# Two residual stages and the projection stripe ahead of each, cut into two token halves, in a hybrid decoder step (Trainium2)

## The reference, cut to what matters

```python
def rmsnorm(x, g):
    x32 = x.astype(F32)
    y = x32 * lax.rsqrt(jnp.mean(x32 * x32, axis=-1, keepdims=True) + EPS)
    return (y * g.astype(F32)).astype(x.dtype)
...
    mix = jnp.concatenate([retention_out(ret_o, rg), diff_head_out(d_o, subln_g, lam_init)], axis=-1).astype(x.dtype)
    x = x + rmsnorm(mix @ w_out, g_mix_post)
    x = x + rmsnorm(cross_attn(rmsnorm(x, g_mem_pre), mem_k, mem_v, w_mem_q, w_mem_o), g_mem_post)
    x = x + rmsnorm(sq_relu_mlp(rmsnorm(x, g_mlp_pre), w_up, w_down), g_mlp_post)
```

## Time and profile before

| | |
|---|---|
| median of 3 runs | 2825.09 us (2824.94 to 2826.55) |
| the profiled execution, its own time | 2828.37 us |
| its span in the trace | 2826.8 us |
| PE busy | 2761.9 us, 98% |
| DVE busy | 2123.9 us, 75% |
| ACT busy | 1115.1 us, 39% |
| TensorE clock granted, mean | 0.994 of full |

### The profile page before, as it was taken

How to read it: one execution, slowest core, us unless ns; L and a number is a source line. 1 busy time by engine, 2 the same in 40 slices (tenths; PEclk the granted TensorE clock), 3 DMA queues, 4 the chain that set the end, 5 groups by cost and what they waited for, 6 DMA issues and landing times.

```text
span 2826.8 us, 48374 instructions
## 1 busy us (share of the span) xinstructions
PE 2761.9 (98%) x18594; PEld 2538.4 (90%) x18594; DVE 2123.9 (75%) x2699; ACT 1115.1 (39%) x1412; POOL 275.8 (10%) x444
## 2 busy tenths in 40 slices
PE   7999999999999999898999999999999999999998
PEld 6999999999899999767899999999988888888887
DVE  7788886665566653757877777777789888888886
ACT  8143333333233332444544444444444333333332
POOL 0000001233312100000000000000010000000000
PEclk9999999999999999999999999999999999999999
DMA  7444345566756554332344444444464433545353
GB/s 236 143 124 135 114 131 173 184 194 190 228 186 227 188 193 134 111 110 91 115 154 136 151 141 144 148 144 138 148 194 134 157 119 117 162 129 159 94 180 134
DMA packets 387959, 430.37 MB, mean 152 GB/s; under 512 B 13878, under 2 KB 300844, under 8 KB 385644
## 3 DMA queue, kind: packets, MB, share of 16 engines
q1 hardware_dynamic: 346088, 269.19, 31.9%
q0 software_dynamic: 41504, 159.26, 16.5%
q10 hardware_dynamic: 228, 0.06, 0.0%
HBM read 342.21 MB, written 86.25 MB: 152 GB/s over the span
## 4 chain that ended last, share of the span: by engine, by line
PE 86%; DVE 8%; issue 2%; DMA 2%; ACT 2%; DVEq 0%; SPq 0%; POOL 0%; ACTq 0%; POOLq 0%
PE gemm L2934 24%; PE gemm L3031 5%; PE aux L3031 5%; PE aux L3033 5%; PE aux L3032 5%; PE gemm L3033 5%; PE gemm L3032 5%; PE gemm L3619 3%; PE gemm L3621 3%; PE gemm L3620 3%; PE aux L3621 3%; PE aux L3620 3%; PE aux L3619 3%; PE aux L3077 2%; PE gemm L3630 1%
## 5 line engine op out<-in xcount | busy, mean ns | idle before, releaser
L2934 PE MATMUL gemm<-act_hi,w_hi 128*128 128x288 f32 x1744 | 390.9, 306 | 3.4 <-DVE act_lo L2400 2.6
L2934 PE MATMUL gemm<-act_hi,w_lo 128*128 128x288 f32 x1744 | 374.2, 296 | 0.0
L2934 PE MATMUL gemm<-act_lo,w_hi 128*128 128x288 f32 x1744 | 373.6, 296 | 0.0
L2934 PEld LDWEIGHTS gemm<-act_hi,w_hi 128*128 128x128 f32 x1744 | 279.5, 189 | 32.0 <-issue 22.0
L2934 PEld LDWEIGHTS gemm<-act_hi,w_lo 128*128 128x128 f32 x1744 | 281.4, 189 | 0.0
L2934 PEld LDWEIGHTS gemm<-act_lo,w_hi 128*128 128x128 f32 x1744 | 281.3, 189 | 0.0
L1700 ACT ACTIVATE w_hi<-w_raw 128x2048 fp32r<-128x2048 f32 x60 | 115.1, 1919 | 304.2 <-PE aux L3621 175.5
L2578 DVE TENSOR_TENSOR w_lo<-w_raw,w_hi 128x1024 fp32r<-128x1024 f32 x120 | 146.7, 1222 | 108.3 <-ACT w_hi L1623 108.3
L1811 DVE TENSOR_TENSOR w_lo<-w_raw,w_hi 128x2048 fp32r<-128x2048 f32 x63 | 144.1, 2287 | 45.7 <-ACT w_hi L1197 45.4
L3031 PE MATMUL gemm<-act_hi,w_hi 128*128 128x288 f32 x504 | 149.9, 298 | 6.9 <-DVE w_lo L1982 4.3
L3031 PE MATMUL aux<-act_hi,w_hi 128*128 128x288 f32 x528 | 155.4, 294 | 0.0
(11 more groups left out here) (522 smaller groups left out, 7694.1 us busy)
## 6 DMA issues: line engine op xcount, KB each, us to landing
w_raw<-in_w_mlp_up SPq DMA_DIRECT2D x120, 512.0 KB, 4.3
w_raw<-in_w_mlp_down SPq DMA_DIRECT2D x32, 1024.0 KB, 6.3
side_hi<-in_w_mlp_down SPq DMA_DIRECT2D x32, 1024.0 KB, 7.1
w_raw<-in_w_in SPq DMA_DIRECT2D x29, 1024.0 KB, 6.6
w_raw<-in_w_in SPq DMA_DIRECT2D x54, 512.0 KB, 4.1
w_raw<-in_w_out SPq DMA_DIRECT2D x16, 1024.0 KB, 5.9
u_sum_scratch<-u_sum POOLq DMA_DIRECT2D x32, 512.0 KB, 2.9
z_scratch<-z_out SPq DMA_DIRECT2D x56, 288.0 KB, 2.4
```

Source lines behind the costliest of these rows:

```text
L2934: ins = M(out[half][:, 0:TH], w[b][:, cols], x[:, k, half * TH:(half + 1) * TH], start=first and n == 0, stop=last and n == 2)
```

## The change

The two stages work by token halves: half 0 is tokens 0 to 287, half 1 the rest. In words:

- The last output tiles before a stage (two before stage 0, four before stage 1: `LAST`) are made by halves: first all of them for half 0, then all for half 1 (`last_tiles`). Between the products of half 1 stand the column sums and the `spread` of half 0's row factor.
- `residual` takes these tiles out of PSUM half by half, and then goes through 32 half-chunks (`q` = 0 to 31, sixteen of half 0, then sixteen of half 1) in place of 16 chunks. `scale`, `add`, `low`, the high part and the square work on 288 tokens each. The loops are written out.
- `col_sums` is called for two of the four quarters at a time: 32 calls for x in a stage in place of 16.
- `root`, `recip` and `spread` run once for each half, four times in a stage in place of two, on 64 of the 128 rows. Those for half 1's y, and those for half 0's new x, stand inside the loop.
- The split of the next weight stripe (`lo_halves`, `hi_halves`) moves from ahead of the loop into its first steps. In stage 1 the split of stripe `S_MLP` on DVE is cut in two and stands between the tiles.
- `behind` becomes 10 half-chunks, in both stages.
- SP's waits for x follow the new counts: the loads after stage 0 still begin after the last `add`, and the first store of x in stage 1 waits for 20 of 32 steps.

```diff
-            def first_tiles(k, stripe, tile, behind):
-
-                col_sums(n_y_sum, n_acc, True, False)
+            def y_sums(k, half):
+
+                groups = range(2 * half, 2 * half + 2)
+                pe.wait_ge(n_yacc, SUM0[k] + KC - LAST[k] + (half + 1) * (LAST[k] - 1))
+                col_sums(n_y_sum, n_acc, True, False, groups)
+                pe.wait_ge(n_ysq, SQ0[k] + KC - LAST[k] + (half + 1) * LAST[k])
+                col_sums(n_y_sum, n_sq[1], False, True, groups).then_inc(n_ss, 1)
+
+            def half_part(b, k, cols, out, half, first, last):
+
+                x = slice(half * TH, (half + 1) * TH)
+                M(out[:, 0:TH], w_hi[b][:, cols], act_hi[:, k, x], start=first, stop=False, skip_group_check=True)
+                M(out[:, 0:TH], w_hi[b][:, cols], act_lo[:, k, x], start=False, stop=False, skip_group_check=True)
+                return M(out[:, 0:TH], w_lo[b][:, cols], act_hi[:, k, x], start=False, stop=last, skip_group_check=True)
+
+            def last_tiles(k, stripe, tile0, ks):
+
+                per, width = LAST[k], 2048 // ks
+                pe.wait_ge(s_wlo, stripe + 1)
                 for half in range(2):
...
+                        for kk in range(ks):
+                            if half and i * ks + kk == 4:
+                                y_sums(k, 0)
+                            elif half and i * ks + kk == 10:
+                                spread(4 * k + 1, 0, n_y_bc)
+                            at = kk * width + j % per * P
+                            ins = half_part(stripe % 2, kk, slice(at, at + P), G[2 * (j % 2) + half], half, kk == 0, kk == ks - 1)
+                        ins.then_inc(s_tile if half else n_h0, 1)
+
+            def first_tiles(k, stripe, behind):
...
+                for q in range(2 * KC):
+                    half, c = q // KC, q % KC
+                    if q == 3:
+                        y_sums(k, 1)
+                    elif q == 7:
+                        spread(4 * k + 2, 1, n_y_bc)
+                    elif q == KC + 5:
+                        spread(4 * k + 3, 0, n_x_bc)
+                    pe.wait_ge(n_xsq, 2 * KC * k + q + 1)
+                    col_sums(n_x_sum, n_sq[c % 2], c == 0, c == KC - 1, range(2 * half, 2 * half + 2)).then_inc(n_used, 1)
+                    if q == behind:
+                        pe.wait_ge(s_wlo, stripe + 2)
+                    if q >= behind:
+                        chunk(1, q - behind)
+                    pe.wait_ge(n_lo, 2 * KC * k + q + 1)
+                    ins = chunk(0, q)
                 ins.then_inc(s_tile, 1)
-                for c in range(KC - behind, KC):
-                    ins = chunk(1, c)
+                for q in range(2 * KC - behind, 2 * KC):
+                    ins = chunk(1, q)
                 ins.then_inc(s_tile, 1)
-                spread(2 * k + 2, n_x_bc)
+                spread(4 * k + 4, 1, n_x_bc)
```

DVE's side of the stage:

```diff
+                for q in range(2 * KC):
+                    if q + 2 == KC:
+                        dve.wait_ge(n_bcs, 4 * k + 2)
+                    if q + 2 < 2 * KC:
+                        scale(q + 2)
+                    low(k, q, g_pre)
+                    if q + 2 < 2 * KC:
+                        add(k, q + 2, g_post)
+                    if q == 0:
+                        y_take_half(k, per - 1, 1, tile0)
+                        y_sum_half(k, per - 2, 1)
+                    elif q == 3:
+                        lo_half(stripe + 1, (stripe + 1) % 2, 0, n_wh, k + 1)
+                    elif q == 4:
+                        lo_half(stripe + 1, (stripe + 1) % 2, 1, s_whi, stripe + 2)
+                    elif q == 5:
+                        recip(4 * k + 2, 1)
+                    elif q == KC + 3:
+                        recip(4 * k + 3, 0)
+                recip(4 * k + 4, 1)
```

More of the change, by code:

```diff
@@ L1457, in spread, with hi_half @@
-            def spread(bc):
-                for half in range(2):
-                    nc.scalar.activation(n_rt[:, half * TH:(half + 1) * TH], bc[half], ACT.Copy).then_inc(n_bcs, 1)
+            def hi_half(n, b, used, part):
+                if part == 0:
+                    act.wait_ge(s_wfull[b], n // 2 * 16 + 16)
+                    act.wait_ge(s_tile, used)
+                cols = slice(part * 1024, (part + 1) * 1024)
+                nc.scalar.activation(w_hi[b][:, cols], w_raw[b][:, cols], ACT.Copy).then_inc(s_whi if part else n_wh, 1)
@@ L1462, in y_square, with root, spread @@
+            def root(half, row_sums):
+                rows = half_rows(half)
+                nc.scalar.activation(n_cr[rows, :], row_sums[rows, :], ACT.Sqrt, bias=eps[rows, :], scale=1.0 / D).then_inc(n_rts, 1)
+            def spread(n, half, bc):
+                act.wait_ge(n_bc, n)
+                nc.scalar.activation(n_rt[:, half * TH:(half + 1) * TH], bc[half], ACT.Copy).then_inc(n_bcs, 1)
             def y_square(j, tile0, b, k):
                 act.wait_ge(s_evac, j + (tile0 + 1))
-                act.wait_ge(n_yacc, max(j - 1, 0) + (k * (KC - 1) + 1))
+                act.wait_ge(n_yacc, max(j - 1, 0) + SUM0[k])
@@ new lines, in recip, with at_step, scale, add @@
+            def recip(n, half):
+                rows = half_rows(half)
+                dve.wait_ge(n_rts, n)
+                V.reciprocal(n_cr[rows, :], n_cr[rows, :]).then_inc(n_rcp, 1)
+            def at_step(q):
+                half, c = q // KC, q % KC
+                return c, slice(half * TH, (half + 1) * TH)
+            def scale(q):
+                c, cols = at_step(q)
+                V.tensor_tensor(yT[:, c, cols], yT[:, c, cols], n_rt[:, cols], ALU.mult).then_inc(n_t, 1)
+            def add(k, q, g_post):
+                c, cols = at_step(q)
+                dve.wait_ge(n_t, 2 * KC * k + q + 1)
+                V.scalar_tensor_tensor(out=xT[:, c, cols], in0=yT[:, c, cols], scalar=gT[:, g_post + c:g_post + c + 1], in1=xT[:, c, cols],
+                                       op0=ALU.mult, op1=ALU.add).then_inc(n_x, 1)
@@ new lines, in low, with residual @@
+            def low(k, q, g_pre):
+                c, cols = at_step(q)
+                dve.wait_ge(n_x, 2 * KC * k + q + 1)
+                dve.wait_ge(n_hi, 2 * KC * k + q + 1)
+                V.scalar_tensor_tensor(out=act_lo[:, c, cols], in0=xT[:, c, cols], scalar=gT[:, g_pre + c:g_pre + c + 1],
+                                       in1=act_hi[:, c, cols].bitcast(F32), op0=ALU.mult, op1=ALU.subtract).then_inc(n_lo, 1)
+            def residual(k, g_post, g_pre, stripe, tile0):
+                per = LAST[k]
+                y_sum(k, KC - per - 1)
+                for i in range(per):
+                    y_take_half(k, i, 0, tile0)
+                    if k and i < 2:
+                        lo_half(stripe, stripe % 2, i, s_whi, stripe + 1)
+                    if i:
+                        y_sum_half(k, i - 1, 0)
+                if k:
+                    y_take_half(k, 0, 1, tile0)
+                recip(4 * k + 1, 0)
+                y_take_half(k, 1 if k else 0, 1, tile0)
+                if k:
+                    y_sum_half(k, 0, 1)
+                dve.wait_ge(n_bc, 4 * k + 1)
+                V.tensor_tensor(yT[:, 0, 0:TH], yT[:, 0, 0:TH], n_y_bc[0], ALU.mult).then_inc(n_t, 1)
@@ L2412, in residual @@
                 add(k, 0, g_post)
[L2413 removed]
+                if k:
+                    y_take_half(k, 2, 1, tile0)
+                    y_sum_half(k, 1, 1)
+                dve.wait_ge(n_bcs, 4 * k + 1)
                 scale(1)
                 add(k, 1, g_post)
[L2416 to L2420 removed]
@@ L3385, in _ @@
             pe.wait_ge(s_retin, 32)
-            for n in range(KC):
+            for n in range(KC - LAST[0]):
                 out_tile(n)
@@ L3547, in _ @@
             ins.then_inc(s_tile, 1)
-            for s in range(1, 4):
+            for s in range(1, 3):
                 pe.wait_ge(s_wlo, S_MO + s + 1)
```

293 lines of the change are left out of this document (141 added, 152 removed).

## The result

The changed kernel takes 2842.02 us (median of 4 runs, 2841.04 to 2843.24), the kernel before 2825.02 us (4 runs, 2824.15 to 2826.55): 17.0 us more. The estimate of the ratio is 1.0054, with a 95% interval of 1.0040 to 1.0067 (the medians by themselves give 1.0060). The forecast was 2832.4, with 2838 as its upper end. The direction is right and the time is above the range.

What follows compares the result with a forecast made beforehand. PE, with DVE almost equal, was taken as the bound, and the two 10.4 us gaps with their low clock as the gain. Stage 0 +4.1 and stage 1 +3.2 gave +7.3 us: 2832.4 for the median, range 2821 to 2838.

Steps and rivals of the forecast that it cites:

- What bounds the kernel: Both stages: PE and DVE almost equal; two gaps of 10.4 us and the low clock behind them are all to gain.
- The prices: Per half-chunk: half sum 0.44 us alone, PE 1.36 with six matmuls; DVE step 1.23; spread of half a factor 0.5.
- The front: Start of stage 0: the gap closes, first product near 1145.5, 8.4 us earlier; tenth `low` at 1160.4.
- The clock should stay full here: Stage 0, after the closed gap: PE's clock stays at its full level.
- rival C: Clock falls inside the stage: three half-chunks behind the tenth at 1.01 us more, both stages, +6: 2838; chance 0.14.
- The main sum: Stage 0 4.1 us longer, stage 1 3.2 longer, +7.3 in all: 2832.4 for the median; chance 0.50.
- A: Half sums among products are cheap, 0.29 us; DVE's chain sets the end: 2826.7, no change; chance 0.16.
- B: Half sums and DVE half steps (1.07 us) both cost by length; stages save 3.8 and 4.6: 2816.7; chance 0.11.
- D: Gap not closed: a late square or sum makes PE wait in half 1; over 2845; chance 0.03.

Runs made afterwards that it cites:

- experiment 8: Kernel before, each chunk's column sum of x in two visits of two quarters with matmuls between them: 2839.23 us, 1.0053 of before.
- experiment 9: Kernel before, each of DVE's three operations of a chunk issued as two of 288 columns: 2835.55 us, 1.0037 of before.
- experiment 4: Kernel before, with filler (matmuls whose result nothing reads), 12 ahead of the spread and 36 behind it in both stages: 2823.15 us, 0.9997 of before.
- experiment 1: Changed kernel, with filler matmuls (nothing reads them) in PE's waits of half-chunks 1 and 3 to 9, both stages: 2832.03 us, 1.0028 of before.
- experiment 2: Changed kernel with filler in half-chunks 1 and 3 to 9, and 28 of each stage's 32 sums of x left out: 2827.46 us, 1.0012 of before.
- experiment 3: Changed kernel without filler, second tile from the sixth half-chunk in place of the tenth, both stages: 2841.99 us, 1.0052 of before.
- experiment 7: Changed kernel, with filler matmuls in half-chunks 1 and 3 to 6 and the second tile from the sixth half-chunk: 2840.24 us, 1.0048 of before.

## Why the prediction was wrong

**What bounds the kernel: half right.** PE and DVE are nearly equal, and what is added to either counts (experiments 8 and 9). But the low clock behind the gap was not something to gain: held at its full level, it moves the ends of the stages by 0.0 and 0.1 us (experiment 4).

**The prices: right.** Half sum 0.44 alone and 0.57 among products (1.36 for a half-chunk, in the changed kernel and in experiment 8). DVE's half step 1.23, and 3.9 and 4.6 us for the halving by itself (experiment 9). Here DVE's fixed cost is larger than in the table of the Trainium skill (VectorE: DVE Perf Modes, the section on the TRN2 errata), 1.23 against the 1.08 estimated from it. The rule there that small tiles pay per tile agrees with the trace: 2.46 us for the two halves of a chunk, 2.13 for the whole one. One small price was off: the spread of half a row factor takes 0.69 us (1177.51 to 1178.20 in experiment 1's trace) and not 0.5.

**The front: right.** The gap is closed, and the first product starts at 1139.62 in a trace that runs 6.0 us ahead: 1145.6, where the forecast had 1145.5. The tenth `low` starts at 1154.44 and 6.0, 1160.4; the forecast had it done by then (it adds 0.9 for `scale` and `low`), so it is 0.5 us later. PE's waits for `act_lo` in half-chunks 4 to 6 are 0.90, 1.33 and 1.20 us, at the lower end of the 1 to 2 that were named; half-chunk 3 has none.

**"The clock should stay full here": wrong, and this is the step that failed.** Two lines on, the prediction leaves PE 0.97 us of work in each step of DVE, and rival C says that 3.3 of DVE's inserted us fall between half-chunks 3 and 7. For the four half-chunks from 3 on that is 3.9 us of work (4 x 0.97) in 8.2 (4 x 1.23 + 3.3), and PE was that thin: 2.81 of 5.40. Against C stood a row with 10.26 of 11.9 us busy, where the clock rose; it was no answer for a stretch with half of that. The row that was near, the gap of the earlier trace rows, with 3.29 of 10.4 us busy and a fall, was taken for C's support and given a chance of 0.14. Behind stage 1 the trace before has a nearer one, which the prediction does not show, with 2.92 of 5.50 us busy, a wait of 2.58 in it, and a fall of 3.4 us from 1401.5:

```profile
1396.00:1401.50 5.50, 2.92 (x23) 2.69 (x22) 5.50 (x6) 0.72 (x1) 0.00 (x0) 1.00 0.00 0
```

What the runs showed in the step's place: 10.2 us at the lower level in each stage, which with the falls elsewhere cost 10.0 us of the 17.0 (experiment 1). The Trainium skill (TensorE: Matmul & The Clock Gate, Part 1) has the clock down for an idle engine; the trace shows that an engine with short waits between its instructions, 2.81 of 5.40 us busy, met the same fate.

**Rival C: right in kind, and nearly right in size for the stages.** It had three half-chunks at 1.01 us more in each stage, 3 us each and 6 in all. At the ends of the stages the low clock cost 2.9 us (8.5 less 5.5) in stage 0 and 3.7 in stage 1. The place was another: in stage 0 the low clock, from 1149.4 on, took in half-chunks 6 to 10 with a spread among them, and not three behind the tenth. The 10.1 us that the filler gives back are 3.3 in stage 0 by the table, 3.7 in stage 1, 1.7 between them and 1.5 in the rest; with half-chunks 5 and 6 alone covered, the two stages give back 3.9 and 4.3. Those 1.7 and 1.5 are two falls of 3.4 us that only the changed kernel's trace has of the two, near 1238 and 2084. The second run of the changed kernel has nothing between the stages and 1.2 more in stage 0, so I cannot say what ties those falls to the stages. They are most of what C's 2838 lacks.

**The main sum by itself** would have been near: 8.4 us behind 1130 us with filler and 7.0 by the medians (2832.03 less 2825.02), for a forecast of 7.3. But that is partly luck, for terms of both signs cancel. With filler stage 0 is 5.5 us longer at its end and not 4.1, and stage 1 5.6 and not 3.7 (5.1 and not 3.2 once DVE's sums have gone on). These are the rows of PE for it, the product of the tenth half-chunk and the next weight's first, in stage 0 and in stage 1:

```profile
1162.08 0.31 PE L3414 MATMUL gemm<-act_hi,w_hi 128*128 128x288 f32 x1
...
1197.83 0.54 PE L2995 MATMUL aux<-act_hi,w_hi 128*128 128x288 f32 x2
...
1342.52 0.30 PE L3414 MATMUL gemm<-act_hi,w_hi 128*128 128x288 f32 x1
...
1378.26 0.54 PE L2995 MATMUL aux<-act_hi,w_hi 128*128 128x288 f32 x2
```

From the one to the other it is 35.7 us in both stages, where the forecast had 35.3: the two spreads. The product itself comes 1.0 us later than forecast in stage 0 (this trace is 0.7 behind) and 1.4 in stage 1 (5.2 behind). A third to a half of that is DVE's tenth `low`. The rest goes with the other fillers: with 5 and 6 alone covered, the product comes 0.4 and 0.6 us later than forecast. Against this stand up to 1.0 us of PE's wait for `c_kc`, which the forecast took as unchanged, and 1.3 in the rest, where the trace before has a fall near 2070 us that the one with filler has not.

**Rivals A, B and D** did not happen. A's other half agrees with experiment 2: with the sums nearly free, DVE's chain keeps the change above the kernel before.

No kernel here beats the one before by more than can be measured; the nearest is the kernel before with filler, 0.9997 [0.9988, 1.0006].

## What to carry to other kernels

Splitting work in halves to close a gap is paid for on every engine whose instructions have a fixed cost: here it closed two gaps of 10.4 us, and its halved sums and steps cost more than closing them gave. Where a change makes PE wait often and briefly, work out PE's busy time in that stretch, and set beside it the rows of the same trace with a share like it and what the clock did behind them. When the clock falls, ask which engine is later: here the low clock cost nothing while DVE was late (experiment 4), and 2.9 and 3.7 us where it made PE the later one. And where the work behind a tile covers the making of the next weight, less of it opens a wait (experiments 3 and 7).
